# Sums of squares for the norms: from products against a column of ones to squares streamed over strips of ones

## The chip, the cores and the metric

The kernel runs on one core of a Trainium2 chip. The metric is the device time of one launch in microseconds (us), all weights read from memory. The core has a matrix engine (TensorE, PE in the rows; its weight loads are PEld), VectorE (DVE), ScalarE (ACT), GpSimd (POOL, which does next to nothing here) and SyncE (SP), which issues the transfers. The engines run beside each other and wait for one another through semaphores.

## The reference, cut to what matters

256 tokens of width 1024 go through a stack in float32: a first layer (mLSTM and differential attention, then a feed-forward part), a second layer (convolution, then a mixture of eight experts), and two more layers of three kinds of attention each. What the change touches are norms over the 1024 features of a token:

```python
def rmsnorm(x, g):
    xf = x.astype(F32)
    y = xf * lax.rsqrt(jnp.mean(xf * xf, axis=-1, keepdims=True) + EPS)
    return (y * g.astype(F32)).astype(x.dtype)

def layernorm(x, g, b):
    xf = x.astype(F32)
    mu = jnp.mean(xf, axis=-1, keepdims=True)
    var = jnp.mean(jnp.square(xf - mu), axis=-1, keepdims=True)
    return ((xf - mu) * lax.rsqrt(var + EPS) * g.astype(F32) + b.astype(F32)).astype(x.dtype)
```

So a token's sum of squares over 1024 features is needed, seven times in the program by the helper that is changed (other norms form their sums in other code).

## The kernel before, in words

**Layout.** An activation is held feature-major: 128 partitions by `KT` = 8 blocks of features by `T` = 256 tokens. A sum over features is therefore a sum over partitions and over the eight blocks, and TensorE makes it.

**Stages.** The program is a row of stages with a barrier between them. A stage built by `project` (L373) is given a list of tasks. A task may have matmuls, which fill a PSUM bank, and has an engine that empties the bank or does a step of its own. Each engine takes its own tasks in the order of the list, so this list is the order of the work on every engine. Weights come as a stream of 1 MB chunks through a ring of nine; SyncE issues a chunk when the one nine earlier has been freed. Banks are given in turn; tasks with fixed banks (`SUM_BANKS`, banks 0 and 1) take those, and in stretches between such tasks the others rotate over the remaining banks only (L398 to L408). Before it fills a bank, TensorE waits until its earlier user has been emptied.

**The norm.** `squares` (L575) has ScalarE square the input, two feature blocks (128x512 values) at a time, in four instructions at L578. `row_sum` (L549) then adds one block: for each half of the tokens, the 128x128 block of squares is the weight that is loaded, and one column of ones is moved over it. It gives the 128 tokens of that half a partition each, a layout in which the following steps have two columns to work on. Each float32 product is two TensorE instructions in the trace, so the eight blocks make 32 of them. `token_rstd` (L557) follows: VectorE scales and adds epsilon (L555), ScalarE takes the root (L562), VectorE the reciprocal (L563). `spread_rows` (L565) then brings the value of each token back to all partitions by two products with the identity, and VectorE multiplies the activation by it in two halves.

**Where it is called.** `squares` is called in seven places: in `modulate` at the end of layer 0's mixing stage (L1334), at the start of the convolution stage (L1395) and at the end of that layer's second stage (L1464); in `center`, the layer norm, at the start of `pw2` (L1437) and at the end of both last layers (L2559); and in the expert layer's final norm at the start of the first of the two last layers (L2409). There four weighting instructions of ScalarE (L2413) stand in the list between the squares and the root, and four behind it. Where outputs are made tile by tile (L1328, L1461, L2557), `row_sum` is called block by block in other loops, and those calls stay as they are.

**Column groups.** A task may be `columned`: its matmuls have 32 weight columns each and go to one of the four groups of columns of the array, so that each writes 32 partitions of a bank. Each group's last matmul counts up a semaphore of its own. `half_sum` (L2176) and the first stage's vector products (L857) work in this way.

Of the kernel before, what the change touches and what calls it, by code (L numbers as in the profile page):

```python
# [16 lines left out]
ALU = mybir.AluOpType  # L17
# [3 lines left out]
P = 128  # L21
D = 1024
KT = D // P
T = 256
# [218 lines left out]
def build(nc, a):  # L243

    ctx = ExitStack()
    with ctx:
# [126 lines left out]
        def project(name, n, tasks, side=None, tail=0, stores=()):  # L373
# [10 lines left out]
            for t in tasks:  # L384
                count[t.engine] += 1
                t.count = count[t.engine]
                if t.side_first:
                    flush = len(fills)
                if t.matmuls:
                    fills.append(t)  # L390
                    t.fill = len(fills)
                    if t.engine == "pe":
                        t.count = t.fill
                    if t.chunk is not None:
                        last[t.chunk] = len(fills)
                    if t.columned and t.chunk is not None:
                        emptied[t.chunk] = t
            fixed = [j for j, t in enumerate(fills) if t.banks]  # L398
            kept = {j for lo, hi in zip(fixed, fixed[1:]) if hi - lo < 24 for j in range(lo, hi)}
# [9 lines left out]
            with Stage(nc, name, ["chain_d", "chain_a", "bank_full", "act_done", "dve_done", "acc_ready", "acc_used0", "acc_used1",  # L409
# [25 lines left out]
                def _(pe):  # L435
                    z = 0
                    for j, t in enumerate(fills):
# [14 lines left out]
                        if t.columned:  # L452
                            for c, final, o, l, r, s, e in t.matmuls(bank, chunk):
                                ins = pe.matmul(o, l, r, start=s, stop=e, tile_position=(0, c))
                                if final:
                                    ins.then_inc(columns[c // 32] if c // 32 in t.columned else bank_full, 1)
# [118 lines left out]
        def squares(add, x, sq, ready):  # L575

            for q in range(KT // 2):
                made = add(None, None, "act", lambda act, bank, link, q=q: nc.scalar.activation(sq[:, 2 * q:2 * q + 2, :], x[:, 2 * q:2 * q + 2, :],  # L578
                                                                                                ACT.Square), ready[q // 2])
                for k in (2 * q, 2 * q + 1):  # L580
                    total = row_sum(add, sq[:, k, :], k, made)
            return total

# [12 lines left out]
        def modulate(add, total, tmp, weight, shift):  # L596

            def scale(h):
                return lambda dve, row: dve.tensor_tensor(tmp[:, h, :], XT[:, h, :], row, ALU.mult)
            made = token_rstd(add, total, EPS)  # L600
            one, two = spread_rows(add, red[:, 2:4], made, (scale(slice(0, KT // 2)), scale(slice(KT // 2, KT))))
# [9 lines left out]
        def center(add, x, sq, total, eps):  # L611
# [12 lines left out]
            total = squares(add, x, sq, ((one,), (two,)))  # L624
            return spread_rows(add, red[:, 2:4], token_rstd(add, total, eps), (scaled(lo), scaled(hi)))

# [318 lines left out]
        def add(*args, **kw):  # L945
            tasks.append(Task(*args, **kw))
            return tasks[-1]
# [193 lines left out]
        def head_out(h):  # L1141
# [10 lines left out]
            def f(dve, bank, link):  # L1152
# [15 lines left out]
                return ins  # L1168
            n_done[h] = add(None, matmuls, "dve", f, tuple(s_done[h]) + tuple(v_ready[h // 4]), serial=True, columned={0: h + 1})

# [924 lines left out]
        for ly in range(LAYERS):  # L2095
# [80 lines left out]
            def half_sum(z, half, need):  # L2176

                def matmuls(bank, chunk):
                    return [(32 * c, r == 3, bank[32 * c:32 * c + 32, 0:P], kb[z][:, 16 * half + 4 * r + c, :], chunk[:, (4 * r + c) * P:(4 * r + c + 1) * P],
                             r == 0, r == 3) for r in range(4) for c in range(4)]  # L2180
                return add(unit(f"c{2 * z + half}")[0], matmuls, "act",
                           lambda act, bank, link: nc.scalar.activation(sums[:, z, half, :], bank[:, 0:P], ACT.Copy), (need,), columned={c: 2 * z + half + 1 for c in range(3)})

# [216 lines left out]
            if ly == 0:  # L2400
# [9 lines left out]
                for k in range(KT):  # L2410
                    if k == 4:
                        rs_made = token_rstd(add, total, EPS)
                    weighted_y = add(None, None, "act", lambda act, bank, link, k=k: nc.scalar.activation(YT[:, k, :], YT[:, k, :], ACT.Copy,  # L2413
# [316 lines left out]
```

## Time and profile before

| what | us |
|---|---|
| median of three runs | 2094.23 (2085.01 to 2284.11) |
| profiled execution, whole | 2092.96 |
| its span | 2090.0 |
| TensorE busy | 1909.3 |
| VectorE busy | 831.9 |
| ScalarE busy | 394.7 |

The mean granted clock of TensorE over the span is 0.935 of full speed. The 2.96 us between span and whole execution lie before the first and behind the last instruction. Busy time is a share of the whole, and says nothing of a single stage: how a norm runs has to be read from the timeline of its few microseconds.

### The profile page before, as it was taken

To read this page: it belongs to the slowest core of one execution; us is meant where nothing else is said; L and a number is where in the kernel's file an instruction comes from. 1 tells how busy PE (TensorE), PEld (TensorE's weight loads), DVE (VectorE), ACT (ScalarE), POOL (GpSimd) and SP (SyncE) were. 2 spreads that over 40 slices of the span, in tenths; PEclk is the share of its full clock that TensorE was granted. 3 is DMA by queue.
4 is the path that set the end of the run, shared out by engine and by line. 5 is a ranking of instruction groups with operands and counts; after the bars stand their busy time and mean duration, and the time that the engine had idled before them with its cause. 6 is when DMAs were issued, how large, how long until landed. Compare 5 with 4: busy or idle time off the path is not lost. (4 is left out here: it accounts for less than half of the span.)

```text
span 2090.0 us, 46368 instructions
## 1 busy us (share of the span) xinstructions
PE 1909.3 (91%) x19691; PEld 1601.9 (77%) x19691; DVE 831.9 (40%) x2262; ACT 394.7 (19%) x1114; POOL 0.5 (0%) x5
## 2 busy tenths in 40 slices
PE   6999887999979877999999999999969998799987
PEld 4677666888868767977889869999658876688766
DVE  3766553778849512011011111111123665236651
ACT  2232332000024221000000000010021233112331
POOL 0000000000000000000000000000000000000000
PEclk7999997999989877999999999999979998899988
DMA  9523242999943024989989899989973421234100
GB/s 393 215 102 122 101 161 74 340 356 367 372 182 141 2 79 175 370 350 419 406 303 384 331 421 418 366 341 352 385 314 122 164 79 61 81 122 161 41 1 20
DMA packets 67922, 480.41 MB, mean 230 GB/s; under 512 B 7424, under 2 KB 9728, under 8 KB 9856
## 3 DMA queue, kind: packets, MB, share of 16 engines
q1 hardware_dynamic: 67712, 477.39, 58.8%
q8 instruction: 158, 2.59, 0.5%
q14 instruction: 52, 0.43, 0.1%
HBM read 476.32 MB, written 1.05 MB: 228 GB/s over the span
## 5 line engine op out<-in xcount | busy, mean ns | idle before, releaser
L461 PE MATMUL PS<-sb_U,sb_ring 128*128 128x256 f32 (+1 forms) x1456 | 383.3, 422 | 19.9 <-PEq L219 13.5
L461 PEld LDWEIGHTS PS<-sb_U,sb_ring 128*128 128x128 f32 x1456 | 288.3, 201 | 102.9 <-issue 63.9
L1637 PE MATMUL PS<-sb_arena,sb_ring 128*64 128x98 f32 x7040 | 305.0, 247 | 10.4 <-issue 8.2
L1637 PEld LDWEIGHTS PS<-sb_arena,sb_ring 128*64 128x64 f32 x7040 | 299.5, 136 | 16.8 <-issue 13.3
L461 PE MATMUL PS<-sb_arena 128*64 128x128 f32 (+9 forms) x884 | 155.2, 353 | 7.3 <-DVE sb_arena L674 4.4
L712 PE MATMUL PS<-sb_U,sb_ring 128*128 128x256 f32 x704 | 155.6, 383 | 6.1 <-PEq L219 6.1
L1653 PE MATMUL PS<-sb_arena,sb_ring 128*64 128x98 f32 x3520 | 156.6, 248 | 1.6 <-issue 1.6
L1653 PEld LDWEIGHTS PS<-sb_arena,sb_ring 128*64 128x64 f32 x3520 | 150.0, 137 | 9.4 <-ACT sb_arena L1918 6.6
L712 PEld LDWEIGHTS PS<-sb_U,sb_ring 128*128 128x128 f32 x704 | 134.5, 192 | 27.2 <-issue 8.8
L461 PEld LDWEIGHTS PS<-sb_arena 64*128 64x128 f32 (+4 forms) x884 | 109.7, 177 | 46.9 <-issue 26.3
L1970 DVE TENSOR_TENSOR sb_arena<-PS,sb_arena 128x98 f32<-128x98 f32 x110 | 28.6, 260 | 291.3 <-ACT sb_arena L1862 291.3
L324 DVE SCALAR_TENSOR_TENSOR sb_arena<-sb_ring,sb_cs,sb_arena 128x256 f32<-128x256 f32 x280 | 135.8, 485 | 10.0
L461 PE MATMUL PS<-sb_consts,sb_arena 128*128 128x1 f32 (+5 forms) x504 | 93.0, 305 | 40.0 <-ACT sb_arena L578 28.0
L461 PE MATMUL PS<-sb_YT,sb_ring 128*128 128x256 f32 x512 | 124.5, 398 | 3.9 <-ACT sb_YT L608 2.0
L1665 PE MATMUL PS<-sb_ring,sb_arena 128*64 128x256 f32 x1056 | 121.2, 382 | 3.9 <-issue 3.8
L461 PEld LDWEIGHTS PS<-sb_consts,sb_arena 128*128 128x128 f32 (+2 forms) x504 | 86.5, 241 | 48.3 <-ACT sb_arena L578 29.9
L461 PEld LDWEIGHTS PS<-sb_YT,sb_ring 128*128 128x128 f32 x512 | 99.1, 199 | 19.2 <-issue 5.9
L1665 PEld LDWEIGHTS PS<-sb_ring,sb_arena 128*64 128x64 f32 x1056 | 75.6, 137 | 40.4 <-issue 6.4
L461 PE MATMUL PS<-sb_ring,sb_U 128*128 128x256 f32 x448 | 101.3, 381 | 0.0
L461 PEld LDWEIGHTS PS<-sb_ring,sb_U 128*128 128x128 f32 x448 | 84.4, 190 | 16.0 <-issue 5.1
L324 DVE SCALAR_TENSOR_TENSOR sb_arena<-sb_ring,sb_small,sb_arena 128x256 f32<-128x256 f32 x168 | 81.5, 485 | 6.0
L1862 ACT ACTIVATE sb_arena<-PS 128x98 f32<-128x98 f32 x110 | 27.9, 254 | 285.4 <-PE PS L1637 285.4
(334 smaller groups left out, 1672.1 us busy)
## 6 DMA issues: line engine op xcount, KB each, us to landing
sb_ring<-stream SPq DMA_DIRECT2D x450, 1024.0 KB, 7.0
sb_consts<-consts SPq DMA_DIRECT2D x1, 1772.5 KB, 27.0
sb_U<-ctxT SPq DMA_DIRECT2D x1, 1024.0 KB, 6.7
sb_XT<-xT SPq DMA_DIRECT2D x1, 1024.0 KB, 8.5
out<-sb_XT SPq DMA_DIRECT2D x8, 128.0 KB, 2.0
sb_small<-small SPq DMA_DIRECT2D x1, 292.0 KB, 2.8
sb_consts<-consts SPq DMA_DIRECT2D x1, 129.0 KB, 2.7
sb_all_small<-layer_small SPq DMA_DIRECT2D x1, 110.0 KB, 27.2
```

The costliest lines, as they stand in the source:

```text
L324: ins = dve.scalar_tensor_tensor(out=o, in0=w[:, :, kt, :], scalar=vec[:, kt:kt + 1], in1=o, op0=ALU.mult, op1=ALU.add)
L461: ins = pe.transpose(o, l, r) if t.turn else pe.matmul(o, l, r, start=s, stop=e)
L712: ins = pe.matmul(PS[:, m % 4, h * T:(h + 1) * T], w[:, h, kt, :], src[:, kt, :], start=(kt == 0), stop=(kt == KT - 1))
L1637: ins = pe.matmul(PS[c:c + 64, m % 4, h * T:h * T + n], w[:, h, kt, c:c + 64], src[:, kt, 0:n], start=(kt == 0), stop=(kt == KT - 1))
L1653: ins = pe.matmul(PS[c:c + 64, 4 + o % 2, 0:n], w[:, c:c + 64], H[:, m, 0:n], start=(m == 0), stop=(m == FT - 1))
L1665: ins = pe.matmul(PS[c:c + HALF, j % 4, 0:2 * P].rearrange("p (n c) -> p n c", n=2), UCT[:, kt, 0:HALF], ws_[z][:, :, kt, :], start=(kt == ...
L1862: nc.scalar.activation(EX[:, m % 2, 0:n], PS[:, m % 4, 0:n], ACT.Silu).then_inc(silu_ready, 1)
L1970: dve.tensor_tensor(H[:, m, 0:n], PS[:, m % 4, T:T + n], EX[:, m % 2, 0:n], ALU.mult).then_inc(hidden, 1)
```

## The change

In the seven calls of `squares`, the sixteen products with a column of ones become eight products with a strip of 32 columns of ones as the weight and a block of squares (128x256) as what moves, in two rounds of four column groups. All four squares are queued first, and TensorE waits for each by `steps`. Each column group ends with 32 equal rows, the sum over its two blocks. ScalarE copies the bank (128x256) into `mean`, and two products with one column of the constant `sel16` (which is one on partitions 0, 32, 64 and 96) both add the four groups and turn the row of tokens into a column. `rstd_of_rows` then does what `token_rstd` did, from two columns of an ordinary bank in place of banks 0 and 1. Apart from this, the counts that columned tasks wait for are now worked out in `project` and no longer written by hand.

```diff
@@ -395,6 +395,11 @@
                         last[t.chunk] = len(fills)
                     if t.columned and t.chunk is not None:
                         emptied[t.chunk] = t
+            finals = [0, 0, 0]
+            for t in fills:
+                for c in t.columned:
+                    finals[c] += 1
+                    t.columned[c] = finals[c]
             fixed = [j for j, t in enumerate(fills) if t.banks]
             kept = {j for lo, hi in zip(fixed, fixed[1:]) if hi - lo < 24 for j in range(lo, hi)}
             turn_of, user = 0, {}
@@ -450,7 +455,9 @@
                         chunk = None if t.chunk is None else ws.chunk(first + main[t.chunk])
                         bank = PS[:, t.banks[0], :]
                         if t.columned:
-                            for c, final, o, l, r, s, e in t.matmuls(bank, chunk):
+                            for i, (c, final, o, l, r, s, e) in enumerate(t.matmuls(bank, chunk)):
+                                if i in t.steps:
+                                    wait_done(pe, t.steps[i])
                                 ins = pe.matmul(o, l, r, start=s, stop=e, tile_position=(0, c))
                                 if final:
                                     ins.then_inc(columns[c // 32] if c // 32 in t.columned else bank_full, 1)
@@ -574,12 +581,24 @@
 
         def squares(add, x, sq, ready):
 
-            for q in range(KT // 2):
-                made = add(None, None, "act", lambda act, bank, link, q=q: nc.scalar.activation(sq[:, 2 * q:2 * q + 2, :], x[:, 2 * q:2 * q + 2, :],
-                                                                                                ACT.Square), ready[q // 2])
-                for k in (2 * q, 2 * q + 1):
-                    total = row_sum(add, sq[:, k, :], k, made)
-            return total
+            made = [add(None, None, "act", lambda act, bank, link, q=q: nc.scalar.activation(sq[:, 2 * q:2 * q + 2, :], x[:, 2 * q:2 * q + 2, :],
+                                                                                            ACT.Square), ready[q // 2]) for q in range(KT // 2)]
+
+            def matmuls(bank, chunk):
+                return [(32 * c, r == 1, bank[32 * c:32 * c + 32, 0:T], ones[:, 0:32], sq[:, 4 * r + c, :], r == 0, r == 1)
+                        for r in range(2) for c in range(4)]
+            rows = add(None, matmuls, "act", lambda act, bank, link: nc.scalar.activation(mean[:, 0:T], bank[:, 0:T], ACT.Copy),
+                       columned=dict.fromkeys(range(3)))
+            rows.steps = {2 * q: made[q] for q in range(KT // 2)}
+            return rows
+
+        def rstd_of_rows(add, rows, eps):
+
+            def matmuls(bank, chunk):
+                return [(bank[:, t:t + 1], mean[:, t * P:(t + 1) * P], const("sel16")[:, 0:1], True, True) for t in range(TT)]
+            t = add(None, matmuls, "dve", lambda dve, bank, link: dve.tensor_scalar(red[:, 0:2], bank[:, 0:2], 1.0 / D, eps, ALU.mult, ALU.add), (rows,))
+            t = add(None, None, "act", lambda act, bank, link: nc.scalar.activation(red[:, 2:4], red[:, 0:2], ACT.Sqrt), (t,))
+            return add(None, None, "dve", lambda dve, bank, link: dve.reciprocal(red[:, 2:4], red[:, 2:4]), (t,))
 
         def add_residual(add, y, rs_made, after=()):
 
@@ -597,7 +616,7 @@
 
             def scale(h):
                 return lambda dve, row: dve.tensor_tensor(tmp[:, h, :], XT[:, h, :], row, ALU.mult)
-            made = token_rstd(add, total, EPS)
+            made = rstd_of_rows(add, total, EPS)
             one, two = spread_rows(add, red[:, 2:4], made, (scale(slice(0, KT // 2)), scale(slice(KT // 2, KT))))
             return [affine(add, "act" if k < 6 else "dve", UX[:, k, :], tmp[:, k, :], weight[:, k:k + 1], shift[:, k:k + 1], one if k < 4 else two)
                     for k in range(KT)]
@@ -622,7 +641,7 @@
             lo, hi = slice(0, KT // 2), slice(KT // 2, KT)
             one, two = spread_rows(add, red[:, 4:6], t, (shifted(lo), shifted(hi)))
             total = squares(add, x, sq, ((one,), (two,)))
-            return spread_rows(add, red[:, 2:4], token_rstd(add, total, eps), (scaled(lo), scaled(hi)))
+            return spread_rows(add, red[:, 2:4], rstd_of_rows(add, total, eps), (scaled(lo), scaled(hi)))
 
         def pointwise(name, steps, prefetch=False):
 
@@ -1166,7 +1185,7 @@
                     if t == 0:
                         link(ins)
                 return ins
-            n_done[h] = add(None, matmuls, "dve", f, tuple(s_done[h]) + tuple(v_ready[h // 4]), serial=True, columned={0: h + 1})
+            n_done[h] = add(None, matmuls, "dve", f, tuple(s_done[h]) + tuple(v_ready[h // 4]), serial=True, columned={0: None})
 
         def norm_chain(x, G, dim, sq, st, need):
 
@@ -2179,7 +2198,7 @@
                     return [(32 * c, r == 3, bank[32 * c:32 * c + 32, 0:P], kb[z][:, 16 * half + 4 * r + c, :], chunk[:, (4 * r + c) * P:(4 * r + c + 1) * P],
                              r == 0, r == 3) for r in range(4) for c in range(4)]
                 return add(unit(f"c{2 * z + half}")[0], matmuls, "act",
-                           lambda act, bank, link: nc.scalar.activation(sums[:, z, half, :], bank[:, 0:P], ACT.Copy), (need,), columned={c: 2 * z + half + 1 for c in range(3)})
+                           lambda act, bank, link: nc.scalar.activation(sums[:, z, half, :], bank[:, 0:P], ACT.Copy), (need,), columned=dict.fromkeys(range(3)))
 
             def whole_sum(needs):
 
@@ -2409,7 +2428,7 @@
                 total = squares(add, YT, sqy, ((), ()))
                 for k in range(KT):
                     if k == 4:
-                        rs_made = token_rstd(add, total, EPS)
+                        rs_made = rstd_of_rows(add, total, EPS)
                     weighted_y = add(None, None, "act", lambda act, bank, link, k=k: nc.scalar.activation(YT[:, k, :], YT[:, k, :], ACT.Copy,
                                                                                                         scale=coef[:, k:k + 1]), (plus[-1],), serial=k == 0)
                 x_halves = add_residual(add, YT, rs_made, (weighted_y,))
```

## Rows read from the trace of the kernel before

**Rows 1.** The page: busy time, then granted clock and GB/s in 40 slices.
```profile
PE 1909.3 (91%) x19691; PEld 1601.9 (77%) x19691; DVE 831.9 (40%) x2262; ACT 394.7 (19%) x1114; POOL 0.5 (0%) x5
...
PEclk7999997999989877999999999999979998899988
...
GB/s 393 215 102 122 101 161 74 340 356 367 372 182 141 2 79 175 370 350 419 406 303 384 331 421 418 366 341 352 385 314 122 164 79 61 81 122 161 41 1 20
```

**Rows 2.** Timeline (start, us, engine, line, operation, count, idle) after layer 0.
```profile
333.14 2.29 ACT L578 ACTIVATE sb_arena<-sb_XT 128x512 f32<-128x512 f32 x4 [4.97 <-DVE sb_XT L593]
...
333.83 6.99 PE L461 MATMUL PS<-sb_consts,sb_arena 128*128 128x1 f32 x32 [4.31 <-ACT sb_arena L578]
340.85 0.16 DVE L555 TENSOR_SCALAR sb_rstd<-PS 128x2 f32<-128x2 f32 x1 [6.60 <-PE PS L461]
...
341.50 1.22 PE L461 MATMUL PS<-sb_consts,sb_rstd 128*128 128x128 f32 x4 [0.69 <-DVE sb_rstd L563]
```

**Rows 3.** Windows: span, length, busy us (count) PE, PEld, DVE, ACT, POOL, PEclk, DMA share.
```profile
333.10:340.85 7.75, 6.99 (x32) 6.90 (x32) 1.15 (x2) 2.29 (x4) 0.00 (x0) 0.50 0.00 0
...
348.80:352.00 3.20, 3.18 (x8) 2.57 (x9) 0.17 (x1) 1.27 (x1) 0.00 (x0) 0.50 0.02 5
352.00:356.00 4.00, 4.00 (x19) 3.50 (x18) 0.00 (x0) 0.00 (x0) 0.00 (x0) 0.94 0.00 0
...
1808.00:1815.00 7.00, 6.00 (x32) 6.00 (x32) 1.42 (x2) 2.28 (x4) 0.00 (x0) 0.64 0.15 62
```

**Rows 4.** Timeline of four other norms: squares to L555.
```profile
709.40 2.28 ACT L578 ACTIVATE sb_arena<-sb_YT 128x512 f32<-128x512 f32 x4 [10.15 <-DVE sb_YT L618]
...
710.64 6.96 PE L461 MATMUL PS<-sb_consts,sb_arena 128*128 128x1 f32 x32 [2.54 <-ACT sb_arena L578]
717.64 0.16 DVE L555 TENSOR_SCALAR sb_rstd<-PS 128x2 f32<-128x2 f32 x1 [7.14 <-PE PS L461]
...
1548.10 2.19 ACT L578 ACTIVATE sb_arena<-sb_YT 128x512 f32<-128x512 f32 x4 [3.56 <-PEq L219]
...
1550.32 1.70 ACT L2413 ACTIVATE sb_YT<-sb_YT,sb_coef 128x256 f32<-128x256 f32 x4
1555.81 0.16 DVE L555 TENSOR_SCALAR sb_rstd<-PS 128x2 f32<-128x2 f32 x1 [6.91 <-PE PS L461]
1556.00 0.20 ACT L562 ACTIVATE sb_rstd<-sb_rstd 128x2 f32<-128x2 f32 x1 [3.98 <-DVE sb_rstd L555]
1556.11 1.69 ACT L2413 ACTIVATE sb_YT<-sb_YT,sb_coef 128x256 f32<-128x256 f32 x4
...
1808.32 2.28 ACT L578 ACTIVATE sb_arena<-sb_arena 128x512 f32<-128x512 f32 x4 [37.44 <-DVE sb_arena L618]
...
1815.15 0.16 DVE L555 TENSOR_SCALAR sb_rstd<-PS 128x2 f32<-128x2 f32 x1 [5.74 <-PE PS L461]
...
2071.22 2.28 ACT L578 ACTIVATE sb_arena<-sb_arena 128x512 f32<-128x512 f32 x4 [37.27 <-DVE sb_arena L618]
...
2078.13 0.16 DVE L555 TENSOR_SCALAR sb_rstd<-PS 128x2 f32<-128x2 f32 x1 [5.81 <-PE PS L461]
```

**Rows 5.** Timeline of L857, column groups of 32, and one window.
```profile
23.37 1.07 PE L857 MATMUL PS<-sb_ring,sb_arena 128*32 128x256 f32 x16 [0.61 <-DMA sb_ring<-stream]
...
29.12 1.93 PE L857 MATMUL PS<-sb_ring,sb_arena 128*32 128x256 f32 x16 [2.19 <-DMA sb_ring<-stream]
...
31.29 0.38 ACT L833 ACTIVATE sb_arena<-PS 128x256 f32<-128x256 f32 x1 [3.74 <-PE PS L857]
...
29.20:30.00 0.80, 0.80 (x12) 0.34 (x16) 0.25 (x1) 0.00 (x0) 0.00 (x0) 0.50 1.07 448
```

**Rows 6.** Line L578: durations of one, min/median/max ns.
```profile
L578 ACT ACTIVATE sb_arena<-sb_XT x12: 612/621/630, 333.1 to 762.0; 128x512 f32<-128x512 f32 x12
```

**Rows 7.** Line L1689's waits for transfers, and one window of the experts.
```profile
  DMA sb_ring<-stream: 24.3, 20
...
1200.00:1300.00 100.00, 93.81 (x1519) 77.92 (x1517) 11.93 (x41) 7.93 (x28) 0.00 (x0) 1.00 1.01 420
```

## The prediction

> **What bounds the kernel now.** I read the page first: TensorE is busy for nine tenths of the span, and in most of the 40 slices its granted clock is full, with dips where the stages meet [rows 1]. So the bulk is matmul work that the change doesn't touch. The question is what the chain of work looks like where a norm is made, and that is read from the timeline there. After layer 0 [rows 2] nothing runs beside the norm: ScalarE squares for 2.29 us, TensorE has 32 short instructions that begin when the first square is there and last 6.99 us, and only then does VectorE begin L555. From the start of the first square to the start of L555 it is 340.85 - 333.14 = 7.71 us, all of it on the path that sets the end, since TensorE has no other task in the list before the norm is spread. ScalarE has made the last square at 2.29; the other 5.4 us are TensorE alone, loading 128 columns of squares for each column of ones.
>
> The clock there is half, 1.2 GHz of 2.4, and it is so through the norm and for 3 us after the next dense work has begun, although TensorE is busy with the row sums for 6.99 of 7.75 us [rows 3]. So the row sums do not hold the clock up now, and to take them away cannot drop it in these places. The two norms at the ends of the last two layers differ: their seven us have a mean of 0.64 [rows 3], so some 2 us of full clock at their start (0.14 / 0.5 x 7).
>
> The stretch from first square to L555, in the seven places: three like that of rows 2 (after layer 0, at the start of the convolution stage, at the end of `pw2`), 7.71 each; the first norm of `pw2`, 717.64 - 709.40 = 8.24; the first of the last two layers, 7.71; and the two layer ends, 6.83 and 6.91 [rows 2, 4]. The sum is 3 x 7.71 + 8.24 + 7.71 + 6.83 + 6.91 = 52.8 us, or 2.5% of the time. That is all that the change can touch, so even a norm sum at no cost would bring little more than 2%.
>
> **The new chain, step by step, at half clock.** The squares themselves stay: 2.29 us until the last is there, and 0.07 until TensorE moves (first square 0.62 us long [rows 6], TensorE 0.69 after its start [rows 2]). Three of four pairs of products can be done before; they wait for their squares, and nothing is behind them that could run.
>
> **The column products.** L857 has the same shape to the letter: eight products of 32 weight columns and 256 moving ones in two rounds of four groups, 16 instructions. Such a burst took 1.07 us at full clock and 1.93 in a stretch where the granted clock was 0.50 [rows 5]. With two rounds at x each at full clock and 2x at half, and a tail c: 2x + c = 1.07 and 4x + c = 1.93, so x = 0.43 and c = 0.21. After the last square only the last two groups' second products remain. If the groups run side by side they take one round: 2 x 0.43 + 0.21 = 1.07 us. Ends: 0.64 us were the clock full (0.43 + 0.21), 1.93 if the whole burst had still to run. I take 1.07.
>
> Here a rule speaks against the change. The rows show that sixteen instructions of 256 moving columns end within 1.93 us at half clock, where one round alone costs 0.86 for two passes, so the groups do overlap. The Trainium skill (TensorE: Matmul & The Clock Gate, Part 3, "What overlaps and what doesn't") says that a weight load overlaps with a running matmul only when its row group differs, and column groups all share their rows. By that rule the products would follow each other; what that gives is the second rival below.
>
> **The copy.** From the end of L857's burst (29.12 + 1.93 = 31.05) to ScalarE's start it is 0.24 us, and its copy of 128x256 from PSUM takes 0.38 [rows 5]. There ScalarE also waits for four groups. Together 0.62. No other ScalarE work is queued there in six places.
>
> **The turn.** After 0.07 us, two products of 128 weight columns and one moving column, four instructions. The 32 of that form took 6.99, so 0.218 each: 0.87 us, and some tail; the four instructions of `spread_rows`, of the same weights and 128 moving columns, took 1.22 [rows 2]. I take 0.95, between 0.87 and 1.22 and nearer the first, whose moving size it has. L555 starts 0.03 after (333.83 + 6.99 = 340.82). Root, reciprocal and spread stay as they are.
>
> Sum: 2.29 + 0.07 + 1.07 + 0.62 + 0.07 + 0.95 + 0.03 = 5.10 us.
>
> **Place by place.** Saved: 3 x (7.71 - 5.10) = 7.83. First norm of `pw2`: 8.24 - 5.10 = 3.14; the extra half microsecond is that row sums must use banks 0 and 1, the spread mean sits in bank 0, and TensorE begins at 710.64, 1.24 after the first square and not 0.69 [rows 4]. The new sum takes the next bank, so that wait goes. Layer ends: (6.83 - 5.10) + (6.91 - 5.10) = 3.54, less because the old row sums ran partly at full clock and the new products' last round begins 2.4 us after the first square, when it has fallen. The first of the last two layers is different: four weighting instructions follow the squares in ScalarE's list. The copy now stands ahead of them, so they wait until 2.19 + 0.07 + 1.07 + 0.62 = 3.95, take 1.70, and the root can start at 5.67 where it started at 7.90 (1556.00 - 1548.10) [rows 4]. TensorE's turn and L555 are done by then (3.95 + 0.07 + 0.95 + 0.03 + 0.16 = 5.16), so ScalarE is what ends last there: saved 2.23. These four instructions had been hidden behind the row sums; that cover is gone.
>
> Total: 7.83 + 3.14 + 3.54 + 2.23 = 16.7 us. The profiled execution took 2092.96, with 2.96 outside its span, which stay: 2076.2. It lies 1.3 below the median of the runs shown, of which the lowest is 8.0 under it, so the run-to-run uncertainty is nearly half of the gain.
>
> **At nothing.** The four waits of TensorE are for squares that it needed before too. Two of the rows' bank restrictions go, so that the convolution stage's tiles rotate over eight banks and not six; no wait of TensorE for a bank shows there, hence no gain. Transfers: SyncE's list is unchanged, and chunks are freed by the tiles, which all come earlier together. The ring is full at each norm before the experts (DMA share 0.00 in rows 3, and 2 and 79 GB/s in the slices ahead of the experts [rows 1]), so a stage that starts earlier finds its nine chunks.
>
> **Bounds.** Per place, at the cheap ends 5.10 - 0.43 - 0.08 = 4.59, at the dear ones 5.10 + 0.86 + 0.27 = 6.23. Over seven: 3.6 us more gain or 7.9 less, so 2073 to 2084.
>
> **Rivals.**
> First, transfers take it back. The experts are near the transfers' pace: DMA share 1.01 in one stretch, and 24.3 us of waits for chunks at L1689 [rows 7]. If chunks' arrival and not TensorE set the experts' end, what is saved in the four places ahead (7.83 + 3.14 = 10.97) is lost, giving 2076 + 11 = 2087. For it: these waits. Against it: the stream is held back by the ring before the experts, so it starts earlier too, and 24.3 us in twenty waits are little in a stage that fills over a dozen slices of 52 us.
> Second, and on the slower side: the column groups do not overlap. Then 16 instructions at 0.43 us each make 6.9 us, from 0.69 after the first square to 7.57; then 0.62 + 0.07 + 0.95 + 0.03 gives 9.24 us, 1.5 us more than before where it was 7.71. Over seven places 7 x 9.24 - 52.8 = 11.9 us slower: 2105. It decides from a burst of 5.35 us on (7.71 - 0.69 - 1.67). Rows 5 speak against it outright; only the waits between the products, which L857 lacks, leave it a small chance.
> Third, the clock. It rises only when dense work has run for a while: 3.2 us at half, then 0.94 [rows 3]. Where it rises shifts with every start. A loss of 16.7 us would need 33 us more at half clock over seven restarts, 4.8 us each, more than the 3.2 now seen after layer 0. It may take or give a few microseconds.
> Fourth, the change does nothing: the row sums would have to be hidden, and rows 2 show no engine at work beside them.
>
> **How the numbers follow.** Forecast, with its own range of 2068 to 2084: 0.80. Transfers 0.06; part of the gain lost to the clock at restarts or to slower copies (2084 to 2092) 0.08; groups one after another 0.02; more gain than the cheap ends, by the clock or by a lower level of all runs (below 2068) 0.04. Range 2066 to 2090. Within 2% (2052 to 2136, about what a measurement of this kernel can tell from no change) 0.96; faster by more 0.03, since the touched 52.8 us would have to vanish nearly whole; slower by more 0.01.
>
> **What the profile after would show.** From first square to L555 5.1 us in six places, among them the first norm of `pw2`; TensorE in two bursts there, the second beginning 0.07 after a copy of 0.38; at the first of the last two layers the root at 5.7, released by ScalarE's own weighting. Dense work after each norm as long at half clock as before. I am wrong if the burst after the last square lasts over 2 us, if ScalarE's copy starts more than half a microsecond after it, or if the experts' waits for chunks grow by what was saved.

## The result, and the profile after

The changed kernel took 2061.99 us at the median of four runs (2057.34 to 2070.22), against 2090.94 for the kernel before; the ratio is 0.989, with an interval of 0.985 to 0.993. Two later comparisons of the same two kernels gave 0.9934 (0.9906 to 0.9962, 12 runs against 35) and 0.9914 (0.9877 to 0.9950, 11 against 17). The ratios and their intervals leave out runs that lie over 1.5% above the fastest of their kernel, as the 2284.11 us of one run of the kernel before does, and so are not the quotients of the medians (0.986 in the first). A gain in us is here the ratio's distance from 1 times the median before: 23.0, 13.8 and 17.9 us. So the change is a gain of 14 to 23 us, or about 1%; by the bound of 2% it is no change.

The profiled execution took 2070.22 us with a span of 2068.4. The page of the kernel after, where [rows 1] has the one before:

```profile
span 2068.4 us, 46226 instructions
...
PE 1886.0 (91%) x19607; PEld 1564.9 (76%) x19607; DVE 832.0 (40%) x2262; ACT 397.1 (19%) x1121; POOL 0.5 (0%) x5
...
PEclk7999997999989777999999999999989998899988
```

TensorE has 84 instructions less (7 x (20 - 32)), and its mean share is the same. What happened is in the timeline. After layer 0 in the kernel after, to be held against [rows 2]; L584 are the squares, L461 the column products, L590 the copy, L599 what L555 was:

```profile
333.69 2.28 ACT L584 ACTIVATE sb_arena<-sb_XT 128x512 f32<-128x512 f32 x4 [5.07 <-DVE sb_XT L612]
...
334.47 2.63 PE L461 MATMUL PS<-sb_arena,sb_consts 128*32 128x256 f32 x16 [4.40 <-ACT sb_arena L584]
...
337.21 0.39 ACT L590 ACTIVATE sb_mean<-PS 128x256 f32<-128x256 f32 x1 [1.23 <-PE PS L461]
...
337.65 1.02 PE L468 MATMUL PS<-sb_consts,sb_mean 128*128 128x1 f32 x4 [0.55 <-ACT sb_mean L590]
338.70 0.16 DVE L599 TENSOR_SCALAR sb_rstd<-PS 128x2 f32<-128x2 f32 x1 [3.91 <-PE PS L468]
...
339.35 1.22 PE L468 MATMUL PS<-sb_consts,sb_rstd 128*128 128x128 f32 x4 [0.69 <-DVE sb_rstd L601]
```

From first square to L599 it is 338.70 - 333.69 = 5.01 us, where it was 7.71. The reader is to see three things. The column products are over 3.41 us after the first square (334.47 + 2.63 - 333.69), which is 1.13 behind the last square: a round, not a burst. The copy begins 0.11 after them. The turn takes 1.02.

The first norm of `pw2` and the first of the last two layers in the kernel after, for [rows 4]:

```profile
706.53 2.28 ACT L584 ACTIVATE sb_arena<-sb_YT 128x512 f32<-128x512 f32 x4 [10.62 <-DVE sb_YT L637]
...
711.53 0.16 DVE L599 TENSOR_SCALAR sb_rstd<-PS 128x2 f32<-128x2 f32 x1 [3.90 <-PE PS L468]
...
1538.50 2.19 ACT L584 ACTIVATE sb_arena<-sb_YT 128x512 f32<-128x512 f32 x4 [3.48 <-PEq L219]
...
1541.93 0.38 ACT L590 ACTIVATE sb_mean<-PS 128x256 f32<-128x256 f32 x1 [1.24 <-PE PS L461]
1542.34 1.70 ACT L2432 ACTIVATE sb_YT<-sb_YT,sb_coef 128x256 f32<-128x256 f32 x4
...
1543.41 0.16 DVE L599 TENSOR_SCALAR sb_rstd<-PS 128x2 f32<-128x2 f32 x1 [4.12 <-PE PS L468]
1543.95 0.19 ACT L600 ACTIVATE sb_rstd<-sb_rstd 128x2 f32<-128x2 f32 x1
```

The first is 5.00 us long (8.24 before). In the second the root starts 5.45 after the first square (7.90 before), right behind the four weightings (L2432, which were L2413), and 0.38 after L599 has ended: ScalarE ends last there. All seven places: 5.01, 5.01, 5.00, 5.01, 5.45 to the root, 5.00, 5.00. Against before that is 3 x 2.70 + 3.24 + 2.45 + 1.83 + 1.91 = 17.5 us less.

The two spans differ by 21.6 us. The other 4.1 lie between the norms, and not where work was changed. From L555 or its successor to the next norm's first square, before and after: 259.4 and 260.7 in the feed-forward stage, 101.4 and 102.2 in the convolution stage, 42.7 and 44.2 in `pw2`, 780.1 and 777.8 in the experts, 252.3 and 247.2 (from the root) in the first of the last layers, and 256.1 and 255.4 in the second. The clock explains the first. The restart after layer 0, a window of the kernel before (columns as in [rows 3]):

```profile
348.82:352.24 3.42, 3.42 (x8) 2.79 (x9) 0.17 (x1) 1.25 (x1) 0.00 (x0) 0.50 0.02 5
```

and two windows of the kernel after:

```profile
346.67:352.70 6.03, 6.03 (x14) 4.85 (x15) 0.17 (x1) 1.25 (x1) 0.00 (x0) 0.50 0.00 0
352.70:356.00 3.30, 3.30 (x16) 2.86 (x15) 0.00 (x0) 0.00 (x0) 0.00 (x0) 0.98 0.02 5
```

Before, dense work began at 348.82, and the clock rose at about 352.5 (the mean of 0.94 from 352 to 356 [rows 3] is half a microsecond at half): 3.7 us at half clock. After, it began 2.15 us earlier, and the clock rose at about 352.8 (0.98 from 352.70 on): 6.2 us at half. So the clock rose at nearly the same point of the execution as before. The 2.5 us more at half clock cost 1.25 us, just what that stretch grew by (1.2). A part of what a norm saves is paid back at once, if the clock does not rise earlier too.

The trace's clock records say how long the clock was at half between the norms. In the convolution stage it was 12.7 us before and 16.8 after, and in `pw2` 8.5 and 13.4: the sign is that of the 0.7 and 1.5 us by which they grew. In the first of the last layers it went the other way, 45.8 us at half before and 37.7 after; this is worth up to 4.0 us of the 5.1 that this stretch lost. In the experts the two are nearly alike (42.8 and 43.9), so the clock does not explain the 2.3 us there.

### The profile page after: what moved, and what is told of

Read it like the earlier page. It is cut to its first block and busy times, and to the rows that moved or that the text cites. A ratio compares the mean times of both kernels' runs of the same rounds, so it can differ in the third digit from the quotient of the medians.

```text
span 2068.4 us, 46226 instructions
## 1 busy us (share of the span) xinstructions
PE 1886.0 (91%) x19607; PEld 1564.9 (76%) x19607; DVE 832.0 (40%) x2262; ACT 397.1 (19%) x1121; POOL 0.5 (0%) x5
## 3 DMA queue, kind: packets, MB, share of 16 engines
HBM read 476.32 MB, written 1.05 MB: 231 GB/s over the span
## 5 line engine op out<-in xcount | busy, mean ns | idle before, releaser
L1656 PEld LDWEIGHTS PS<-sb_arena,sb_ring 128*64 128x64 f32 x7040 | 299.4, 136 | 16.7 <-issue 12.9
L751 PE MATMUL PS<-sb_arena,sb_ring 128*128 128x256 f32 x352 | 78.5, 382 | 0.0
L2058 DVE COPY sb_arena<-PS 98x128 f32<-98x128 f32 x40 | 11.7, 292 | 158.6 <-PE PS L1788 158.6
```

The costliest lines, as they stand in the source:

```text
L751: ins = pe.matmul(PS[:, 4 + o % 3, 0:T], w[:, (b % BLOCKS) * P:(b % BLOCKS + 1) * P], H[:, m, :], start=(m == 0), stop=(m == FT - 1))
L1656: ins = pe.matmul(PS[c:c + 64, m % 4, h * T:h * T + n], w[:, h, kt, c:c + 64], src[:, kt, 0:n], start=(kt == 0), stop=(kt == KT - 1))
L2058: dve.tensor_copy(YC[0:n, o % 2, :], PS[0:n, o % 2, 0:P]).then_inc(yc_copied, 1)
```

## The experiments

The rival theories: **A**, the seven shortened stretches are the gain, and the rest is how the clock happened to stand in that execution. **B**, there is a further systematic gain in other stages. And for the terms of the sum: what the overlap of the groups is worth, what of the burst is exposed, and what the bank wait was.

### The same kernel again (e1, e9)

No edit. Expected of e1:

> The changed kernel once more, to see how large the gain is and what beyond the seven norms belongs to it. In the two profiles the stretch from the first square to L555 (at the first of the last two layers: to the root) is shorter by 3 x 2.70 + 3.24 + 2.45 + 1.83 + 1.91 = 17.5 us in sum. Theory A (the norms are all of it, and what is over in the first comparison, 23 us of 2091, is how the granted clock happened to stand in the last layers): 17 to 18 us, a ratio of 0.9915 within 0.003, and among executions of one kernel the span goes with the mean granted clock. Theory B (a systematic further gain in other stages, by banks, transfers or clock): 22 us or more again, ratio 0.9895 or lower.

Expected of e9:

> The changed kernel a third time, beside e10 and e11 on the same chip. By theory A and by e1 it is 14 to 17.5 us faster than before: a ratio of 0.9915 to 0.9935.

Measured: e1 0.9934 (0.9906 to 0.9962), 13.8 us of 2088.3, less than the 17 to 18 that A gave, but A's ratio is inside the interval; e9 0.9914 (0.9877 to 0.9950), 17.9 us of 2083.8. Both profiles have the seven stretches of the first to 0.01 us. Theory A is enough for the times; B's ratio of 0.9895 or lower is outside e1's interval, though inside e9's. Beside e1, single runs of the kernel before go from 2070.8 to 2106.8. In the first four runs after, span and mean clock went together: 2068.4 at 0.937, 2061.1 and 2059.3 at 0.941, 2055.6 at 0.945.

What lies between the norms is not the same in every execution. After layer 0 in e9, two windows:

```profile
343.30:346.50 3.20, 3.20 (x8) 2.57 (x9) 0.16 (x1) 1.24 (x1) 0.00 (x0) 0.50 0.00 0
346.60:350.00 3.40, 3.40 (x18) 2.99 (x17) 0.00 (x0) 0.00 (x0) 0.00 (x0) 1.00 0.02 5
```

Dense work begins at 343.30 there and runs at half for 3.2 us only, as before the change. Over the kept profiles of this section and the next, the stretches between the norms in us, with the time at half clock from the clock records in brackets:

| stretch | before | e2 | e3 | after | e1 | e9 |
|---|---|---|---|---|---|---|
| feed-forward stage | 259.4 (17.1) | 260.7 (21.7) | 259.2 (16.9) | 260.7 (21.7) | 260.6 (21.7) | 259.2 (16.9) |
| convolution stage | 101.4 (12.7) | 102.1 (16.8) | 101.4 (12.7) | 102.2 (16.8) | 102.1 (16.8) | 102.3 (17.0) |
| experts | 780.1 (42.8) | 784.4 (50.5) | 781.6 (37.5) | 777.8 (43.9) | 784.4 (47.2) | 778.5 (44.7) |
| first of the last layers | 252.3 (45.8) | 252.3 (45.8) | 247.5 (38.0) | 247.2 (37.7) | 247.4 (37.9) | 251.5 (46.7) |

In the first two stages the norm ahead is new in e2, after, e1 and e9, in the last row in e3, after, e1 and e9. So it is not all chance. The convolution stage is longer by 0.7 to 0.9 us wherever its norm is new, the feed-forward stage by 1.2 to 1.5 in three of four, and the first of the last layers is shorter by about 5 in three of four. This last is a piece of what B asks for, and where it comes it comes with 8 us less at half clock. The largest scatter is that of the experts, 777.8 to 784.4 us; it doesn't go with the norms, the clock doesn't explain it, and its cause stays open.

### Only four, only three (e2, e3)

```diff
+            place[0] += 1
+            if not (place[0] <= 4):      # e3: place[0] > 4
+                return squares_by_rows(add, x, sq, ready)
```

`squares_by_rows` is the old function, and where it was used the old `token_rstd` follows. Only a part of the diff is shown, and the comment in it gives e3's version of the line.

> The new sum in the four places before the experts (after layer 0, start of the convolution stage, both norms of pw2), the old row sums in the three behind. Theory A: 3 x 2.70 + 3.24 = 11.3 us faster than before, ratio 0.9946. Rival (transfers in the experts take back what is gained ahead of them): ratio 1.000 within 0.002. Theory B with its extra in the last layers: the same 11.3.

> The new sum in the three places behind the experts only. Theory A: 2.45 + 1.83 + 1.91 = 6.2 us faster than before, ratio 0.9970. Theory B (the extra is made in the last layers): 11 us or more, ratio 0.9945 or lower. Rival with the transfers: here all of the gain of the change, ratio 0.99.

Measured: e2 0.9929 (0.9903 to 0.9955), 14.8 us; e3 0.9968 (0.9943 to 0.9993), 6.7 us. The stretches in the profiles (e2's is that of its longest execution, 2088.9 us) are those of the new kernel where it is new (5.0) and those of the old one elsewhere (7.71, 6.84, 6.92 in e2). So the gain ahead of the experts arrives at the end: the rival that the transfers would take back 11 us is refuted, since a ratio of 1.000 is outside the interval. What e3 gains is what its three stretches give (6.2); B's 11 us lie just inside the edge of its interval (0.9943 is 11.9 us), so B is made unlikely by it and not refuted. The two sum to 21.5 us where the whole change gave 13.8 beside them; with intervals of 5 us and more each that is no contradiction, and it is no finer than that.

### All products in one column group (e4)

```diff
-                return [(32 * c, r == 1, bank[32 * c:32 * c + 32, 0:T], ones[:, 0:32], sq[:, 4 * r + c, :], r == 0, r == 1)
-                        for r in range(2) for c in range(4)]
+                return [(bank[0:32, 0:T], ones[:, 0:32], sq[:, k, :], k == 0, k == KT - 1) for k in range(KT)]
...
```

Not shown of the diff: the task is no longer `columned`, and the copy and the turn work on 32 rows.

> The changed kernel with its eight column products all in one group of 32 columns, accumulated one after the other; ScalarE copies 32 rows, the turn sums one row. If it is the overlap of the four groups that makes the burst short, 16 instructions at 0.43 us follow each other: the burst ends 7.6 us after the first square and not 3.4, the stretch is 9.2 us, and the whole is 7 x 4.2 = 29 us slower than the changed kernel, some 6 to 12 us slower than before. If column groups do not overlap in any case (the rival of the prediction), it takes as long as the changed kernel.

Measured: 0.9961 (0.9936 to 0.9986), faster than before where 6 to 12 us slower was expected, and only 5.6 us slower than e1 beside it, not 29; the two intervals overlap. The timeline after layer 0 in e4, and two windows of it:

```profile
332.10 2.29 ACT L584 ACTIVATE sb_arena<-sb_XT 128x512 f32<-128x512 f32 x4 [4.97 <-DVE sb_XT L610]
...
332.88 6.04 PE L468 MATMUL PS<-sb_arena,sb_consts 128*32 128x256 f32 x16 [4.40 <-ACT sb_arena L584]
...
338.95 0.37 ACT L589 ACTIVATE sb_mean<-PS 32x256 f32<-32x256 f32 x1 [4.57 <-PE PS L468]
...
339.38 0.60 PE L468 MATMUL PS<-sb_consts,sb_mean 32*128 32x1 f32 x4 [0.46 <-ACT sb_mean L589]
340.02 0.16 DVE L597 TENSOR_SCALAR sb_rstd<-PS 128x2 f32<-128x2 f32 x1 [6.81 <-PE PS L468]
...
340.67 0.71 PE L468 MATMUL PS<-sb_consts,sb_rstd 128*128 128x128 f32 x4 [0.69 <-DVE sb_rstd L599]
...
332.88:337.50 4.62, 4.62 (x11) 1.92 (x12) 0.33 (x1) 1.51 (x3) 0.00 (x0) 0.50 0.00 0
338.00:340.50 2.50, 1.52 (x9) 0.74 (x7) 0.21 (x2) 0.57 (x2) 0.00 (x0) 1.00 0.00 0
```

The stretch is 7.92 us (7.17 to 8.18 in the seven places) and not 9.2, and over the seven places 53.4, that is 18.5 more than the new kernel's 34.9 (both up to the step after the turn, L597 and L599, also in the first of the last layers, where that is 4.91). The overlap of the groups is worth this much of the chain, and the rival of the prediction, by which the groups don't overlap, is refuted: with one group sixteen instructions take 6.04 us, in four groups the same sixteen take 1.93 at half clock when they run in one burst (e5 below). But in one group they did not take 6.9 either. The clock was 0.50 up to 337.5 and 1.00 from 338.0 on: about 5 us after 256-wide products began it rose, and the turn (0.60) and the spread (0.71) ran at full clock. The old row sums, 6.99 us of instructions with one moving column each, left it at half in the same place [rows 3]. Over the execution e4's mean clock is 0.949 and e1's 0.936, which is 212 us at half against 265 by the clock records (twice the missing share of the span). Most of the 18.5 us came back between the norms: against e1's profile the three stages that follow the first norms are 3.8 us shorter in sum, and the second of the last layers 9.3 (27.3 us at half and not 48.3). A further 6.8 us lie in the experts, and are no more than what executions differ by there.

### All four squares first (e5)

```diff
-            rows.steps = {2 * q: made[q] for q in range(KT // 2)}
+            rows.steps = {0: made[-1]}
```

> The changed kernel, but TensorE waits for all four squares before its first column product, so the whole burst of 16 instructions stands behind the last square. By the prediction's term (one round of 1.07 us behind the last square, 1.93 for a whole burst) each stretch grows by 0.86, from 5.0 to 5.9 us. If instead the burst's length in the stretch were set by something else than the clocked passes (the waits between products, say), it grows by less than 0.4.

Measured: one run, 2072.61 us. In the timeline after layer 0 in e5, the first line is the last of the four squares:

```profile
332.69 0.61 ACT L584 ACTIVATE sb_arena<-sb_XT 128x512 f32<-128x512 f32 x1
...
333.45 1.93 PE L461 MATMUL PS<-sb_arena,sb_consts 128*32 128x256 f32 x16 [6.05 <-ACT sb_arena L584]
...
335.55 0.38 ACT L590 ACTIVATE sb_mean<-PS 128x256 f32<-128x256 f32 x1 [2.25 <-PE PS L461]
...
337.03 0.16 DVE L599 TENSOR_SCALAR sb_rstd<-PS 128x2 f32<-128x2 f32 x1 [4.91 <-PE PS L468]
```

The burst is 1.93 us, as L857's at half clock [rows 5], and stands whole behind the last square. The seven stretches are 5.87 to 6.02, longer by 0.9 to 1.0 and not by 0.86: the burst ends 2.08 behind the last square (333.45 + 1.93 - 333.30), where the new kernel's last round ends 1.13 behind it. TensorE begins 0.15 us after the last square here, and ScalarE's copy 0.17 us after the burst (335.55 - 335.38) where it was 0.11. So the term was right in kind: what is exposed in the new kernel is one round, and its passes set it.

### Bank 0 (e6)

```diff
-                       columned=dict.fromkeys(range(3)))
+                       columned=dict.fromkeys(range(3)), banks=(0,))
```

> The changed kernel with the column products fixed to bank 0, so that at the first norm of pw2 they wait as the old row sums did for VectorE's second half, and the tiles near the norms rotate over six banks again. If the wait for bank 0 was what the 8.24 us there had over 7.71, and the products have room to catch up before the last square (they have: 1.2 us of waiting and one round of 0.9 end before 2.3), every stretch stays at 5.0 and the tiles show no new wait. If the bank matters in itself, the stretch at the first norm of pw2 is 5.5.

Measured: one run, 2066.13 us, all stretches 4.98 to 5.01 (4.98 in the first of the last layers, with the root at 5.45 as without the edit). At the first norm of `pw2` in e6:

```profile
705.80 2.28 ACT L584 ACTIVATE sb_arena<-sb_YT 128x512 f32<-128x512 f32 x4 [10.60 <-DVE sb_YT L637]
...
706.96 2.25 PE L461 MATMUL PS<-sb_arena,sb_consts 128*32 128x256 f32 x16 [2.44 <-ACT sb_arena L584]
...
709.32 0.38 ACT L590 ACTIVATE sb_mean<-PS 128x256 f32<-128x256 f32 x1 [1.24 <-PE PS L461]
...
710.81 0.16 DVE L599 TENSOR_SCALAR sb_rstd<-PS 128x2 f32<-128x2 f32 x1 [3.90 <-PE PS L468]
```

The products begin at 706.96, 1.16 after the first square: the wait for bank 0 is back, as [rows 4] had it. It costs nothing, since the burst ends 1.13 us after the last square all the same and the stretch is 5.01. The half microsecond of before was paid because the row sums had no slack; now there is some.

### Extra wide products (e7, e8, e11) and a square on VectorE (e8, e10)

e7, in `spread_rows`, a task of TensorE alone behind the spread:

```diff
+            add(None, lambda bank, chunk: [(bank[:, 0:512], ones, consts[:, 0:512], True, True) for _ in range(6)], "pe", None)
```

e10, in `squares` (the list of ScalarE's squares ends at `range(3)` there, which is not shown; e8 is e7 and e10 together; e11 is e10 with three such products behind the residual's spread and two behind that of `modulate`):

```diff
+            made.append(add(None, None, "dve", lambda dve, bank, link: dve.tensor_tensor(sq[:, 6:8, :], x[:, 6:8, :], x[:, 6:8, :], ALU.mult), ready[1]))
```

> The changed kernel, and behind each pair of spreading products TensorE makes six products of 128 weight columns of ones and 512 moving columns of constants into a bank nobody reads (extra work, no result), while VectorE works. One group of columns (e4) showed the clock at full from 5 us after wide products began, where row sums left it at half for 7. Theory C (the norms cost more than their chain, since dense work after each runs at half clock for 3 to 6 us and the chain's own products too): the granted half-clock time of the whole falls from 228 us by a third or more, the four products of the turn and the spread take 0.6 and 0.7 us and not 1.0 and 1.2, and the whole is 10 to 20 us faster than the changed kernel. Rival: the extra products (5.2 us at half clock) are still running when VectorE or ScalarE is done, and what the clock gives is lost again: the same time or up to 8 us slower.

> As e7, and the last two of the eight blocks are squared by VectorE (128x512, a product of the input with itself) while ScalarE squares the second and third pair. ScalarE's three squares end 1.75 us after the first begins, VectorE's begins when its second half is made (1.13) and takes about 0.6: the squares are ready 0.5 us earlier, the stretch is 0.5 shorter than in e7 in all seven places, 3.5 us in sum. Rival: VectorE's square takes 1.2 us as its other 128x1024 steps do, and nothing is gained.

> The changed kernel with the last two blocks squared by VectorE, without extra products. e8's profile shows VectorE's square of 128x512 taking 0.69 us and ending 1.82 us after ScalarE's first square begins, where ScalarE alone ends at 2.29. Each stretch is 0.45 us shorter (4.55), 3 us in sum: ratio to before 0.0015 under that of e9, which the times can hardly tell, so the stretches in the profile decide. Rival: the DVE square comes late in the first of the last two layers, where four small steps stand before it (about 0.9 us), and gives the same 4.5 there; none of the others is touched.

> As e10, with three extra products of 512 moving columns behind the residual's spread and two behind the spread of modulate, none in the layer norms (e7 had six everywhere: they ran into the column products there, 8.3 us at the first norm of pw2, and into the barrier of the next stage). Theory C: half-clock time falls by 20 us or more against e10 and the whole is 3 to 8 us faster than e10. Rival: so few products don't raise the clock, and the time is that of e10.

Measured: e7 0.9973 (0.9947 to 0.9999), e8 0.9966 (0.9931 to 1.0001). Neither was run beside the new kernel, but against the kernel before each gained less than e1 and e9 did (the intervals overlap), and neither shows the 10 to 20 us that theory C gave. After layer 0 in e7:

```profile
329.76 6.75 PE L468 MATMUL PS<-sb_consts 128*128 128x512 f32 x12
...
333.60 2.28 ACT L585 ACTIVATE sb_arena<-sb_XT 128x512 f32<-128x512 f32 x4 [4.88 <-DVE sb_XT L613]
...
336.44 1.07 PE L461 MATMUL PS<-sb_arena,sb_consts 128*32 128x256 f32 x16
...
338.15 0.61 PE L468 MATMUL PS<-sb_consts,sb_mean 128*128 128x1 f32 x4 [0.63 <-ACT sb_mean L591]
338.79 0.16 DVE L600 TENSOR_SCALAR sb_rstd<-PS 128x2 f32<-128x2 f32 x1 [4.09 <-PE PS L468]
...
340.45 6.53 PE L468 MATMUL PS<-sb_consts 128*128 128x512 f32 x12
...
348.75 7.58 PE L732 MATMUL PS<-sb_U,sb_ring 128*128 128x256 f32 x34 [1.77 <-PEq L219]
```

Theory C was right on the clock and wrong on the time. The clock rises at 332.65 by the clock records, some 3 us after the extra products begin, the turn takes 0.61 us, and the mean clock of the execution is 0.958, 176 us at half where the new kernel had 261 at 0.937. But the twelve instructions last 6.75 us here and 6.53 behind the second spread, and run into the column products (which then come in one burst at 336.44, 2.84 after the first square) and into the barrier (the next stage begins at 348.75 and not at 346.67). The 5.2 us that was expected is twelve times 0.43, the price at half clock of an instruction with 256 moving columns; these have 512. And the 228 us from which the expectation let the half-clock time fall is not that of the new kernel's profile, which is 261. At the first norm of `pw2`, where the gap is only 2.0 us, the stretch was 8.31. The rival named this, and it decided.

In e8 the granted clock was higher still (0.963), VectorE's square took 0.69 us, and the seven stretches are 39.5 us in sum where e7's are 42.2. That is 2.7 less and not 3.5, and it is not the same in every place: in both layer ends it is 6.14 in e7 and in e8, because there the extra products, and not the squares, end last.

e10 and e11 were run beside e9: 0.9905 (0.9864 to 0.9945) and 0.9898 (0.9857 to 0.9938), against e9's 0.9914. After layer 0 in e10:

```profile
333.79 1.76 ACT L584 ACTIVATE sb_arena<-sb_XT 128x512 f32<-128x512 f32 x3 [5.10 <-DVE sb_XT L613]
...
334.56 2.35 PE L461 MATMUL PS<-sb_arena,sb_consts 128*32 128x256 f32 x16 [4.40 <-ACT sb_arena L584]
334.93 0.69 DVE L586 TENSOR_TENSOR sb_arena<-sb_XT 128x512 f32<-128x512 f32 x1
...
338.52 0.16 DVE L600 TENSOR_SCALAR sb_rstd<-PS 128x2 f32<-128x2 f32 x1 [2.90 <-PE PS L468]
```

VectorE's square ends 1.83 us after the first square begins, and the stretch is 4.73, shorter by 0.28 and not by 0.45. The column products end 1.29 us after that square and not 1.13. A likely reason, not tested, is that the third and fourth pair are now ready together, so that all four groups' second products stand behind them and not two. Over seven places at half clock 0.28 is 2 us. One place is different, the norm at the end of the first of the last layers, a window of e10:

```profile
1780.60:1784.33 3.73, 2.33 (x20) 1.05 (x20) 1.79 (x2) 2.14 (x4) 0.00 (x0) 1.00 0.18 77
```

That norm ran wholly at full clock, with no extra product, and took 3.73 us. In e11, after layer 0:

```profile
333.71 1.77 ACT L584 ACTIVATE sb_arena<-sb_XT 128x512 f32<-128x512 f32 x3 [4.98 <-DVE sb_XT L614]
...
334.48 1.73 PE L461 MATMUL PS<-sb_arena,sb_consts 128*32 128x256 f32 x16 [0.53 <-ACT sb_arena L584]
...
337.44 0.16 DVE L600 TENSOR_SCALAR sb_rstd<-PS 128x2 f32<-128x2 f32 x1 [1.91 <-PE PS L468]
...
338.10 0.71 PE L468 MATMUL PS<-sb_consts,sb_rstd 128*128 128x128 f32 x4 [0.69 <-DVE sb_rstd L602]
...
344.91 4.61 PE L734 MATMUL PS<-sb_U,sb_ring 128*128 128x256 f32 x10 [3.39 <-PEq L219]
```

Here the short fill is over before the first column product, the stretch is 3.73, the spread takes 0.71 at full clock, and dense work begins at 344.91 where it began at 346.67. It was so in the three places that have extra products just ahead of the norm (3.73 to 3.75). The four others have none ahead, the clock was at half for at least a part of each, and the stretches were 4.72, 4.73, 4.72 and 4.58; among them is the one that e10 ran at full clock. Against e9 neither e10 nor e11 is told apart by the times (a difference of 0.001 to 0.002 with intervals of 0.004 on each side): they may be better by some 2 us, and nothing here shows it but the stretches. Theory C's 3 to 8 us between e11 and e10 did not come: the medians are 2065.8 and 2062.8, although e11's mean clock over its six runs is 0.946 and e10's over seven 0.941, some 20 us less at half.

## Why the prediction was right, step by step

**The bound.** It read 52.8 us as all that the change can touch, and so put nearly all chance within 2%. That held.

**The column products.** One round at half clock exposed, from L857's two rows. Measured 1.13 behind the last square where 0.07 + 1.07 = 1.14 was forecast; e5 exposed the whole burst and found its 1.93. The Trainium skill (TensorE: Matmul & The Clock Gate, Part 3, "What overlaps and what doesn't") lets a weight load overlap with a running matmul only where the row group differs; read as saying that products in column groups follow each other, it would have made it 6.9 us. The traces do not bear that reading out for float32: sixteen instructions take 1.93 us at half clock in four groups (e5), and 6.0 us in one (e4), the last part of it at full clock.

**The copy.** 0.24 us of lag was taken from L857 and L833; it was 0.11, so the two stood at 0.50 and not 0.62. That is the largest error of a term; L857's lag goes with a burst that runs whole, and e5, whose burst does so, has 0.17. The four semaphores that ScalarE waits for cost nothing that shows.

**The turn.** 0.95 taken between 0.87 and 1.22; 1.02 measured, or 1.05 from its start to L599 with the step behind it. The errors cancel in part: 5.01 for 5.10 forecast.

**The first of the last layers.** That the four weightings lose their cover, and ScalarE ends last: so it was, with the root at 5.45 (5.67 forecast).

**The bank.** That the wait for bank 0 goes was right, that its going is what saves the half microsecond was not: e6 puts it back and nothing is lost. It is the slack behind the first products that took it away.

**The sum.** 16.7 us forecast; 17.5 in the seven stretches of the profiles; 13.8, 17.9 and 23 us in the three comparisons. In absolute terms the first median, 2062.0, lies 4 us under the range of 2066 to 2090, while 2071.6 and 2064.4 were later seen, one in the range and one under it. So of the first comparison's time only a part is what the prediction explained. The range was centred on one profiled execution of the kernel before, at 2092.96; the three usual runs beside the first result have a median of 2087.65, and later medians were 2083.8 to 2088.3. This level is 5 us of the 14 between the forecast 2076.2 and 2062.0, the stretches are 0.8, and some 8 are how the four runs stood, which twelve runs (2071.6) did not repeat. The outcome under 2068 had been given 0.04; e1's, with more runs, is in the range.

**The rivals.** Transfers: refuted by e2, and by the profile, where L1689's waits for chunks are 24.3 us before and (as L1708) after. Groups one after the other: refuted by e4 and e5. The clock: it was given a few microseconds either way, and did take 1.2 us after layer 0 and give up to 4 in the first of the last layers. Its price was named rightly. What was wrong is the sign "dense work after each norm as long at half clock as before": after layer 0 it was 6.2 us for 3.7. That an earlier start can leave the rise where it is was not seen, nor that the clock can rise within a norm, as it did in e4.

## What to carry to other kernels

When a stage stands alone on the path, add up the stretches that a change can touch before anything else: here 52.8 us of 2093 bounded the answer before a single price was known. Of products that wait for what another engine makes one after the other, only those behind the last one count, so split the work into groups that run side by side and start them as their inputs arrive; a wait for a bank or an input early in the burst is then free. And look for a burst of the same shape elsewhere in the same trace, at both clocks: two such rows priced the column products to 0.01 us, and the lag of the copy behind them to 0.13.

## What the runs showed of the hardware that was not expected

- Sixteen float32 instructions of 32 weight columns and 256 moving columns took 1.07 us in four column groups at full clock and 1.93 at half; in one group, 6.04 us, of which the last part was at full clock.
- 32 instructions with one moving column, 6.99 us on end, left the granted clock at half. Behind sixteen with 256 moving columns it rose about 5 us after they began (e4), and behind twelve with 512 after some 3 us (e7), in the same place of the program (e7's had fallen only just before they began).
- The start of dense work 2.15 us earlier moved the rise of the clock not earlier but about 0.3 us later; in three further profiles with the new norm after layer 0 (e1, e2, e6) it also rose between 352.1 and 353.0, but in e9 at 346.5. Executions of one kernel differed by 13 us in span with a mean clock between 0.937 and 0.945.
